# A hybrid encoder step on one core: the turn between its two parts rebuilt around a sample tile of two products

## The reference

```python
proj = rmsnorm(x, norm_g) @ w_in
aq, ak, av, ag, gq, gk, gv, gg, glr, cv, cgl, cg = split(proj)
# attention (8 heads on 2 kv heads, band of 128 past frames and the chunk's 64, ALiBi, a sink)
y_attn = band_attention(rmsnorm(q), rmsnorm(k), v, sinks) * silu(ag)
# gated linear attention (GLA): 4 heads, chunks of 64 with a carried state S
log_a = log_sigmoid(glr @ gla_w_up + gla_b) / 16
b = cumsum(log_a);  q_t = q * exp(b);  k_t = k * exp(-b)
o = tril(q_t @ k_t.T) @ v + q_t @ S
S = exp(b_last) * S + (k * exp(b_last - b)).T @ v
y_gla = rmsnorm(o, gla_g) * silu(gg)
# causal depthwise convolution of 31 taps over 256 channels
c = conv(cv * sigmoid(cgl)) + conv_b
y_conv = (silu(layernorm(c)) @ w_pw + b_pw) * silu(cg)
return x + concat(y_attn, y_gla, y_conv) @ w_out
```

## Time and profile before

| | |
|---|---|
| median of 3 runs | 953.91 us (952.09 to 954.38) |
| profiled execution | 955.08 us, span 953.3 us |
| busy PE / weight loads (PEld) | 912.0 / 806.2 us |
| busy DVE / ACT / POOL | 787.7 / 474.5 / 202.3 us |
| granted TensorE clock, mean | 0.99 of full speed |

### The profile page before, as it was taken

The page is one execution under the profiler, slowest core; times in us unless marked ns, Lnnn a source line. Parts: engine busy times, 40 slices in busy tenths (PEclk is TensorE's granted clock), DMA queues, the critical chain, the costliest instruction groups (busy, mean ns, idle before and its releaser), DMA issues.

```text
span 953.3 us, 15957 instructions
## 1 busy us (share of the span) xinstructions
PE 912.0 (96%) x5713; PEld 806.2 (85%) x5713; DVE 787.7 (83%) x1905; ACT 474.5 (50%) x1166; POOL 202.3 (21%) x250
## 2 busy tenths in 40 slices
PE   5879999999999999999899999999999999999987
PEld 5667888888888888887897987989999898999965
DVE  6877888888888888889889889888788888878974
ACT  7666766677676676668672251331514233151411
POOL 1332222222221222220021330211203011120410
PEclk9999999999999999999999999999999999999989
DMA  9532222332333332135333221121120402112021
GB/s 306 197 120 92 105 103 88 109 111 101 110 111 111 111 111 89 67 117 152 102 113 100 68 68 65 47 78 56 45 89 1 125 9 78 56 45 90 1 78 58
DMA packets 57839, 87.79 MB, mean 92 GB/s; under 512 B 10048, under 2 KB 34496, under 8 KB 57760
## 3 DMA queue, kind: packets, MB, share of 16 engines
q1 hardware_dynamic: 57760, 86.77, 27.7%
HBM read 60.21 MB, written 26.60 MB: 91 GB/s over the span
## 4 chain that ended last, share of the span: by engine, by line
PE 76%; DVE 13%; ACT 5%; DMA 3%; issue 2%; SPq 1%; POOLq 0%; DVEq 0%; POOL 0%; ACTq 0%
PE J L667 21%; PE J L1892 18%; PE J L682 9%; PE J L2060 7%; DVE acc L1526 5%; PE J L2045 4%; PE S L1947 3%; PE T L1982 1%; PE T L2142 1%; ACT whi L469 1%; ACT sc L1013 1%; PE S L2214 1%; DVE wlo L479 1%; DMA x_normed_scratch<-xraw 1%; PE J L2082 1%
## 5 line engine op out<-in xcount | busy, mean ns | idle before, releaser
L1526 DVE SCALAR_TENSOR_TENSOR acc<-ub,cwh,acc 128x256 f32<-128x256 f32 (+1 forms) x480 | 221.2, 525 | 0.2
L667 PE MATMUL J<-whi,xhi 128*128 128x512 f32 (+1 forms) x408 | 151.0, 370 | 10.8 <-DVE wlo L479 9.7
L1892 PE MATMUL J<-xbh,whi 128*128 128x256 f32 (+1 forms) x512 | 150.6, 294 | 2.7 <-DVE xbl L535 0.9
L667 PE MATMUL J<-wlo,xhi 128*128 128x512 f32 (+1 forms) x408 | 147.2, 361 | 0.0
L667 PE MATMUL J<-whi,xlo 128*128 128x512 f32 (+1 forms) x408 | 147.0, 360 | 0.0
L1892 PE MATMUL J<-xbh,wlo 128*128 128x256 f32 (+1 forms) x512 | 146.2, 286 | 0.0
L1892 PE MATMUL J<-xbl,whi 128*128 128x256 f32 (+1 forms) x512 | 145.3, 286 | 0.3 <-DVE xbl L535 0.3
L1892 PEld LDWEIGHTS J<-xbh,whi 128*128 128x128 f32 x512 | 97.2, 190 | 7.2 <-issue 4.7
L1892 PEld LDWEIGHTS J<-xbh,wlo 128*128 128x128 f32 x512 | 97.3, 190 | 0.2
L1892 PEld LDWEIGHTS J<-xbl,whi 128*128 128x128 f32 x512 | 96.8, 190 | 0.5 <-issue 0.5
L667 PEld LDWEIGHTS J<-whi,xhi 128*128 128x128 f32 x408 | 78.1, 191 | 21.7 <-DVE xlo L625 9.7
(11 more groups left out here) (270 smaller groups left out, 2251.6 us busy)
## 6 DMA issues: line engine op xcount, KB each, us to landing
out<-res SPq DMA_DIRECT2D x60, 256.0 KB, 2.0
x_normed_scratch<-xraw SPq DMA_DIRECT2D x17, 512.0 KB, 2.9
xraw<-xT SPq DMA_DIRECT2D x16, 512.0 KB, 3.5
xtok<-in_x_prompt SPq DMA_DIRECT2D x16, 512.0 KB, 3.6
res<-in_x_prompt SPq DMA_DIRECT2D x16, 512.0 KB, 4.4
xbraw<-x_normed_scratch SPq DMA_DIRECT2D x16, 512.0 KB, 5.2
res<-out SPq DMA_DIRECT2D x14, 512.0 KB, 4.1
wraw<-in_w_in SPq DMA_DIRECT2D x52, 128.0 KB, 2.5
```

What stands on the lines that cost most here:

```text
L667: last = nc.tensor.matmul(bank[:, 0:width], x[x_slot(ps, t)][:, k, :], w, start=(k == 0 and n == 0), stop=(k == KT - 1 and n == 2))
L1526: nc.vector.scalar_tensor_tensor(acc[:, j, 0:frames], src, w, acc[:, j, 0:frames], ALU.mult, ALU.add).then_inc(conv_step, 1)
L1892: last = nc.tensor.matmul(bank[:, 0:w], wt, x[:, k, 0:w], start=(k == 0 and m == 0), stop=(k == KT - 1 and m == 2))
```

## The change

The sample tile's 64 tokens fill both halves of one stationary operand: the high parts of x in columns 0 to 63 and the low parts in 64 to 127. Two products (by w.hi and by w.lo) replace three. Its results come in two halves of the bank, which GpSimd adds (`add_high`, `add_rest`, `add_rest_b`) after ScalarE has moved the lower half out. The same holds for its two outputs. Scores, exponentials, transposes and P times V of the sample tile are done for one chunk of queries and not two. The start of the kernel loads x in two halves and puts tile 1's chunk 0 earlier. In the turn weight splits move on ScalarE and VectorE; one half of x of pairs 0 to 2 and six output weights are split by GpSimd. x of pair 1 has a buffer of its own (`xb1raw`) and is loaded sooner. The taps 0 of pairs 0 and 1 and the LayerNorm scaling of all pairs but the last go to ScalarE. The first half of the GLA scores and the gate logits now use 128 columns and 128 rows.

```diff
-                             ("wup", P, LR + 1), ("sts", GH * GV, P)):
+                             ("wup", P, P), ("sts", GH * GV, P)):
...
+        def split_lo_too(a, b):
+            for n, (part, k, what, col, width) in list(enumerate(B.pieces))[a:b]:
+                nc.gpsimd.wait_ge(B.whi, n + 1)
+                hi, lo = weights(col, width)
+                nc.gpsimd.tensor_tensor(lo, stage(stage_of(B, n))[:, 0:width], f(hi), ALU.subtract).then_inc(B.wlo, 1)
...
+        def chunks_of(t):
+            return (0,) if t.n == LAST else (0, 1)
...
+        def load_x_half(i):
+            ks = half_of_k(i)
+            nc.sync.dma_start(xraw[0][:, ks, :], xT_p[0, :, ks, :]).then_inc(A.x_loaded[0] if i == 0 else consts_b, 16)
...
+            elif b == 1:
+                nc.sync.wait_ge(B.wlo, 4 * KT)
...
+        def split_pair_lo_too(b, i):
+            nc.gpsimd.wait_ge(xb_hi, tile_no(b, i) + (0 if b == 1 else 1))
...
         def evacuate(t, c, dst, bank):
+            if t.n == LAST:
+                if c == 2:
+                    nc.scalar.wait_ge(*taken(t, 0))
+                nc.scalar.activation(low_part(c), bank[DEC:P, :], ACT.Copy, scale=rinv[DEC:P, t.n:t.n + 1])
+                nc.scalar.activation(dst[0:DEC, :], bank[0:DEC, :], ACT.Copy,
+                                     scale=rinv[0:DEC, t.n:t.n + 1]).then_inc(A.taken[c], 1)
...
+        def add_high(t, c, dst):
+            nc.gpsimd.wait_ge(A.taken[c], t.n + 1)
+            nc.gpsimd.tensor_tensor(dst[0:DEC, :], dst[0:DEC, :], low_part(c), ALU.add).then_inc(A.taken[c], 1)
...
-                for n, (x, w) in enumerate(((xhi, hi), (xhi, lo), (xlo, hi))):
+                products = ((xhi, hi), (xhi, lo), (xlo, hi))[0:2 if t.n == LAST else 3]
...
+        def add_rest_b(h):
+            nc.gpsimd.wait_ge(o_low, 2 * TILES + 2 + h + 1)
+            nc.gpsimd.wait_ge(B.out_added, 2 * 2 + h + 1)
+            for n, part in enumerate((on[0:DEC, 2, :], gvt[0:DEC, 2, :])):
...
-            load_x(Tile(0, 0))
-            load_weights(sp, A, 0, KT)
+            load_x_half(0)
+            load_weights(sp, A, 0, 2)
+            load_x_half(1)
+            load_weights(sp, A, 2, KT)
...
+                if b == 1:
+                    split_lo_too(4 * KT, 4 * KT + 6)
+                    pool.wait_ge(B.wlo, 4 * KT + 6)
                 for g in groups(b - 1) if b < NB else []:
                     ln_rinv(g)
...
+                if b == 0:
+                    split_pair_lo_too(1, 1)
+                    add_rest(0)
+                    add_rest(1)
+                if b == 1:
+                    split_pair_lo_too(2, 1)
+                    add_rest_b(0)
+                    add_rest_b(1)
...
+                if t.n == LAST - 1:
+                    split_hi(B, 0, 2)
...
-                if t.n == LAST - 1:
-                    split_hi(B, 0, STAGES)
...
+                    if t.n == LAST - 1:
+                        split_hi(B, 2, STAGES)
...
-                if t.n == LAST - 1:
-                    split_hi(B, STAGES, 2 * STAGES)
...
+            def first_tap(b):
...
+            def ln_scale(g):
+                gi, _, w, own = g
...
+                act.wait_ge(ln_r, gi + 1)
+                act.wait_ge(yg_lo, gi + 1)
+                for n, i in enumerate(own):
+                    last = nc.scalar.activation(cn[rows, i, :], bank[rows, 256 * n:256 * n + 256], ACT.Identity,
+                                                scale=rs[rows, i:i + 1], bias=nmr[rows, i:i + 1])
...
+                first_tap(0)
...
+                split_pair_hi(1, 1)
+                split_pair_hi(1, 0)
+                take_rest(0)
+                take_rest(1)
...
-                conv(0, 24, 30)
+                conv(0, 24, 27)
+                split_pair_lo(1, 0)
+                state(0, 0)
+                conv(0, 27, 30)
                 add_out(A, Tile(0, LAST), 0, bank_of("outa", LAST, 0))
-                state(0, 0)
-                split_pair_lo(1, 0)
                 conv(0, 30, 32)
-                add_out(A, Tile(0, LAST), 1, bank_of("outa", LAST, 1))
                 state(0, 1)
                 mask_scores(0, 2)
-                split_pair_lo(1, 1)
+                add_out(A, Tile(0, LAST), 1, bank_of("outa", LAST, 1))
...
-                conv(0, 36, 40)
-                state(0, 2)
+                conv(0, 36, 41)
                 o_norm(g)
                 history(1)
                 glu(1, 0)
+                conv(0, 41, 45)
+                state(0, 2)
+                conv(0, 45, 48)
                 o_sums(sample)
...
-                split_lo(B, OUT_LO, OUT_LO + STAGES)
...
-                split_lo(B, OUT_LO + 4, OUT_LO + 6)
+                logit_parts(1)
                 ln_stats(g)
                 ln_stats(sample)
-                logit_parts(1)
-                ln_scale(g)
                 y_lo(sample, on_y(sample), ybg, 4.0, yg_hi, yg_lo)
-                ln_scale(sample)
...
                     project(A, B0, 0, empty_bank("in", B0.n, 0))
+                    project(A, B0 + 1, 0, empty_bank("in", 1, 0))
...
-                first = kbs[:, 0, :] if i == 2 else kb[:, i, 0, :]
-                last = nc.tensor.matmul(by_head(bank[0:64, 0:256]), first, qbd[:, :, i * P:i * P + CHUNK], start=True,
+                rows = slice(0, DEC if i == 2 else P)
+                first = kbs[:, 0, :] if i == 2 else kb[:, i, 0:2, :].rearrange("p c n -> p (c n)")
+                last = nc.tensor.matmul(by_head(bank[rows, 0:256]), first, qbd[:, :, i * P:i * P + CHUNK], start=True,
...
                 output(A, Tile(0, LAST), 1, empty_bank("outa", LAST, 1))
-                gla_o(0, 1)
-                scores(0, 2)
-                state_update(0, (2,))
...
                 project_b("cgl", b, 0)
                 if b == 1:
+                    gla_o(0, 1)
+                    scores(0, 2)
+                project_b("cv", b, 0)
+                if b == 1:
+                    state_update(0, (2,))
+                project_b("cgl", b, 1)
+                if b == 1:
                     gla_o(0, 2)
```

More of the change, by code:

```diff
@@ L317, in build @@
         rs = sb("rs", [P, 3])
+        nmr = sb("nmr", [P, 3])
         cn = on
@@ L680, in output @@
                 hi, lo = weights(col, 512)
-                for n, (y, w) in enumerate(((yhi, hi), (yhi, lo), (ylo, hi))):
+                products = ((yhi, hi), (yhi, lo), (ylo, hi))[0:2 if t.n == LAST else 3]
+                for n, (y, w) in enumerate(products):
                     last = nc.tensor.matmul(bank[:, :], y[:, k, :], w, start=(k == 0 and n == 0),
-                                            stop=(k == 3 and n == 2))
+                                            stop=(k == 3 and n == len(products) - 1))
             last.then_inc(ps.out_psum, 1)
@@ L730, in empty_bank @@
             if n >= 3 and (kind, b, i) != ("out", NB - 1, 3):
-                nc.tensor.wait_ge(*emptied(*ORDER[n - 3]))
+                before = ORDER[n - 3]
+                nc.tensor.wait_ge(*emptied(*before))
+                if before[0:2] == ("outa", LAST):
+                    nc.tensor.wait_ge(o_low, 2 * TILES + before[2] + 1)
+                if before[0:2] == ("out", 0) and before[2] >= 4:
+                    nc.tensor.wait_ge(o_low, 2 * TILES + 2 + before[2] - 3)
             return bank_of(kind, b, i)
@@ L1184, in conv_silu @@
                     cth_ready, 1)
+            def ln_scale(g):
+                gi, _, w, own = g
+                rows = slice(0, min(w, P))
+                bank = T[2] if own == (2,) else S[0]
+                act.wait_ge(ln_r, gi + 1)
[3 more added lines that the diff above has]
+                                                scale=rs[rows, i:i + 1], bias=nmr[rows, i:i + 1])
+                last.then_inc(cn_ready, 1)
             def y_hi(g, src, dst, scale, ready, done):
@@ L1345, in scores_max @@
                 def scores_max(n):
-                    for c in range(2):
+                    for c in chunks_of(t):
                         u = 2 * n + c
@@ L1512, in conv @@
                 frames = UB - HIST if b == 0 else 256
-                for n in range(a, e):
+                base = conv_steps(b)
+                by_act = CJ if b < 2 else 0
+                for n in range(max(a, by_act), e):
                     tap, j = n // CJ, n % CJ
@@ L1857, in _ @@
                     if b == 1:
-                        conv(b, 37, 48)
+                        conv(b, 37, 40)
+                        add(p, 2, 0)
+                        conv(b, 40, 44)
+                        add(p, 2, 1)
+                        conv(b, 44, 48)
                 else:
@@ L2049, in output_b @@
             def output_b(b, i, h):
-                at = WIDE - P if i == 2 else i * P
+                high, low = i * P, y_low_at(i * P)
                 bank = empty_bank("out", b, 2 * i + h)
@@ L2057, in output_b @@
                     hi, lo = weights(W_OUT + k * D + h * 512, 512)
-                    yh, yl = (ybg, ybc)[k // 2]
```

(13 more changed lines are left out.)

336 lines of the change are left out of this document (233 added, 103 removed).

## The result

The changed kernel takes 959.1 us (median of 8 runs, 956.13 to 960.39) where the kernel before takes 952.64 (8 runs): ratio 1.0054, 95% interval 1.0040 to 1.0069. Slower by half a per cent, where 1.6% faster was forecast. Timed again beside its variants, it took 955.57 against 951.84, ratio 1.0037 (1.0021 to 1.0054).

A forecast was written before the change was run, and what follows sets the result against it. TensorE bounds the steady attention tiles and part B pairs, VectorE nearly bounds the turn. Terms -1.7 - 6.0 + 1.5 - 2.8 - 7.0 = -16.0 take the profiled 955.1 to 939.1, median 938 us; range 924 to 947.

The forecast's parts named there:

- part 3 of the prediction: Turn, 506 to 594 us: GpSimd takes VectorE's work; 1.5 us lost up to 549, then 2.8 us gained.
- price of the lock: VectorE taps beside GpSimd in the turn: blocking costs VectorE 1.4 of 1.91 us, seven tenths of GpSimd's span.
- the walk: VectorE's list followed in order through the turn to 549 us: TensorE's 6 us gain given back, 1.5 more lost.
- the lock in full: Rival: 18 us of added GpSimd spans hit VectorE whole, 5 us more, clock 2 more; 946 us, chance 0.15.
- Start: Kernel start: x in halves, first matmul at about 6.5 us instead of 9.7; 1.7 us gained, 0.3 to 3.5.
- Sample tile: Sample tile of two products, up to 506 us: fewer projections, scores and transposes; 6.0 us gained, 3 to 9.
- 506 to 594: The turn with work moved to GpSimd: 1.5 us lost from 506 to 549, 2.8 gained from 549 to 594.
- The switch of shape: Part B after 594 us: wider scores and gate logits save 1.07 us a pair; 7.0 us gained, 1 to 8.
- slower: Turn: ScalarE's queue waits for GpSimd splits and delays TensorE; priced waits of 8.4 us must grow 16 more; chance 0.06.

The follow-up runs named there:

- experiment 1: Changed kernel with all low parts that GpSimd makes from pair 1 on (x of pairs 1 and 2, six output weights) back on VectorE: 953.13 us, ratio 1.0006.
- experiment 7: Changed kernel with only the low parts of the six output weights back on VectorE: 954.46 us, ratio 1.0011.
- experiment 11: Kernel of experiment 10 with gated y of pair 0 and normed o of the sample moved ahead of four weight splits and three taps: 946.39 us, ratio 0.9936.
- experiment 8: Kernel of experiment 3, with GpSimd also splitting the second half of x in each steady pair (3 to 7): 950.43 us, ratio 0.9970.
- experiment 5: Kernel of experiment 3 with the sample's output in part B back to three products, without the ScalarE copies and four GpSimd adds: 946.58 us, ratio 0.9929.
- experiment 12: Kernel of experiment 4 plus the change's start (x of tile 0 in halves, earlier tile 1 loads, table load under first load): 948.41 us, ratio 0.9954.
- experiment 9: Kernel of experiment 4 plus one unused buffer of 3 elements a partition, so everything behind it lies at other addresses: 945.32 us, ratio 0.9919.
- experiment 4: Kernel before with only the wider first half of the GLA scores and gate logits of 128 rows: 947.18 us, ratio 0.9953.
- experiment 2: Changed kernel with LayerNorm scaling of all pairs and first taps of pairs 0 and 1 back on VectorE; GpSimd's splits stay: 953.53 us, ratio 1.0011.
- experiment 3: Changed kernel with GpSimd's splits, LayerNorm scaling and first taps all back on VectorE: 950.23 us, ratio 0.9976.
- experiment 10: Kernel of experiment 5 without the two small unused buffers the change added (`minus`, `nmr`): 948.77 us, ratio 0.9954.

## Why the prediction was wrong

**The turn from 506 us on (part 3 of the prediction) failed, by its price of the lock and by where the walk stopped.** From the logits of pair 0 to those of pair 2 the trace has 13 us more than before, where the prediction had a gain. It took "1.4 us of 1.91 are lost, seven tenths" from the earlier trace rows. The row can be read otherwise, and the later traces bear that out: GpSimd's second operation took 1.04 us where the first took 0.87, as it would if it waited for a tap that had slipped into the gap of 0.08 between them. GpSimd's recorded span then holds its own wait, and of the time in which it worked VectorE got nothing. With four splits back to back no tap slips in: the loss was 5.5 us, about their 4.91 and the rest of a root together, and not 0.85 for each. By the prediction's price the four would have cost 3.4 us and saved 2.6. In experiments 1 and 7 the wait before the sample's transposes falls from 7.7 to 4.6 us without them; the 4.6 left, which the forecast had as 5, go to 0.8 when two steps of VectorE are moved (experiment 11).

The Trainium skill, SBUF — State Buffer, Who interferes with whom, calls the shared pair of ports an exclusive lock, and says that a VectorE instruction with two inputs in SBUF contends with a GpSimd one that reads SBUF, and that one with at most one such input, outside its two-port modes, does not. The traces agree (5.5 us, 2.2 us, and in experiment 8 2.68 us for one split and 0.43 for the reads of PSUM), and the prediction gave it 0.15.

Even so the rival "the lock in full" came to 946 us only. It lacked the second thing: the walk along VectorE's list ended at 549 us, and 549 to 594 was written as 2.8 us gained, with 0.5 us for blocking. VectorE is late at 607 us, where TensorE stands 5.1 us before the conv transposes of pair 1, a wait that the prediction does not have. Without the four adds of the sample's output on GpSimd it is 1.6 (experiment 5): they cost two rows of taps 0.9 us each, and the 1.9 us of matmuls that they save TensorE are spent waiting. The split of pair 2 is not the cause: it costs a row of taps 1.6 us and saves 1.1, and without it the wait is 5.2 (experiment 1). And behind the long waits came half clock, 2.6 and 1.6 us in the trace, where the prediction had only taken one away.

By its terms, in the profiled executions:

- **Start**, -1.7 forecast: -2.3 in the trace at tile 2, not seen in the medians (experiment 12).
- **Sample tile**, -6.0 forecast: of 7.0 us at pair 0's logits 2.3 are the start, and 1.9 come in the thirteen tiles behind it, nearly all of them by the address effect (1.6 in experiment 9); 2.8 remain, just under its lower bound of 3. Waits of TensorE from 418 to 460 us grew from 2.7 to 5.7 (2.0 before part B's first projection, 1.4 for score maxima, 0.9 for a low half of P). The last two are waits for VectorE; what ended the first the profile does not show, and no run tried which move made them.
- **506 to 594**, -1.3 forecast (+1.5, -2.8): +6.2 from pair 0's logits to pair 1's, and 1.2 more until pair 2's projections begin (590.30 us, before 589.89). The wait for the sample's transposes that was forecast at 5 us was 7.7.
- **The switch of shape**, 1.07 a pair: right. Each score step is 0.43 and the logits are 0.43 in the chain of the changed kernel:

```profile
695.89 0.43 PE T L2426 x2
696.32 0.43 PE T L2429 x2
696.75 0.43 PE S L2426 x2
697.18 0.43 PE S L2429 x2
```

Alone it gives 1.09 a pair (experiment 4). In the changed kernel 0.8 came, since the shift of addresses takes 0.28 (experiment 9), in the five pairs behind the wait at 607.

These terms are of the two traces, which are 1.0 us of span apart. The rest of the 3.7 to 6.5 us that were measured lies in executions that were not profiled, most of them with a lower mean clock than the kernel before has; no trace shows where in the kernel.

The forecast of "slower" (0.06) was for ScalarE's queue; what happened was another mechanism, VectorE's queue behind GpSimd. The part on ScalarE mattered too: with the scaling and taps back there are 2.5 to 4 us less (experiments 2, 3), part of it in the clock. Which wait it goes back to, the traces do not show.

The cause is settled as far as this: undoing the splits, the scaling with the taps, and the pair output's two products moves the ratio from 1.0037–1.0054 to 0.9929. The kernel before with the width alone reaches 0.9953, with the width and the shift 0.9919, as good as the best version of the whole change (0.9913). So the rest of the change, start, sample tile and turn, is worth nothing that these runs can tell. What is shown is the cost of GpSimd's four splits and of its adds; the cost of the part on ScalarE is shown as a time, and its mechanism is open.

## What to carry to other kernels

Work moved from VectorE to GpSimd is not off VectorE where GpSimd reads SBUF beside VectorE operations with two inputs in SBUF: charge VectorE the whole GpSimd time that falls beside such operations, and take it as free only beside VectorE's reads of PSUM (here 5.5 us lost beside four splits, 2.2 beside one of x, 1.6 where the split began beside such reads). Where two engines are both nearly full, walk the list of the second to the next place where the first waits for it, however far behind the edit: a gain of the first engine is given back there, and half clock can come on top. Of a large change time the smallest local part alone; here the wider scores and gate logits by themselves reached 0.9953, and with the shift of addresses 0.9919, as good as the best version of the whole.

## What the hardware showed that was not expected

The same TensorE instructions had another pitch when all buffers behind one of 12 bytes a partition lay elsewhere: 12 matmuls of 512 columns 2.79 us instead of 2.75, a pair 54.81 instead of 54.53, and an attention tile 25.1 instead of 25.2, with one value in the four kernels without the shift (experiments 4, 10, 11, 12; the tiles of the kernel before too) and the other in all those with it. Which operand's address does it was not tried.

Nor does one kernel show one clock. In the two profiles of the changed kernel the same 24 matmuls take 5.42 and 4.32 us behind the same wait of 7.7, the next 48 take 7.27 and 5.79 behind waits of 1.2 and 1.3, and 48 output matmuls 6.48 and 7.88 behind 5.1. A gain of 1 or 2 us that one trace shows behind a wait is no effect of the edit until other executions show it.
